# A two-block decoder on one core: expert gates made for 128 second keys at once, in groups of 4 tokens

## The reference, cut to what matters

```
choice:  128 triples (n1, n2, g) for each token: 8 heads x 16, g the softmax share
y[t]  =  sum over the triples of  g * gelu(h[t] . down[n1, n2]) * up[n1, n2]
x     =  x + y
```

## Time and profile before

| | us |
|---|---|
| median of three runs | 2606.18 (2598.7 to 2606.22) |
| the profiled execution | 2596.85 |
| its span | 2594.8 |
| PE busy | 2501.0 (96%) |
| DVE busy | 1346.8 (52%) |
| ACT busy | 418.4 (16%) |
| POOL busy | 237.9 (9%) |
| moved by DMA | 642.19 MB, mean 247 GB/s |

### The profile page before, as it was taken

How to read it: one execution, slowest core, us unless ns; L and a number is a source line. 1 busy time by engine, 2 the same in 40 slices (tenths; PEclk the granted TensorE clock), 3 DMA queues, 4 the chain that set the end, 5 groups by cost and what they waited for, 6 DMA issues and landing times.

```text
span 2594.8 us, 36855 instructions
## 1 busy us (share of the span) xinstructions
PE 2501.0 (96%) x15378; PEld 2095.0 (81%) x15378; DVE 1346.8 (52%) x2630; ACT 418.4 (16%) x1206; POOL 237.9 (9%) x256
## 2 busy tenths in 40 slices
PE   8999999999998899999999999889999999999998
PEld 7558999999988765699999999878666677776665
DVE  5825788888744385188888785434500010451001
ACT  2121121110110122122211011102100000430000
POOL 0000113222211000002311121100000000000000
PEclk9999999999999999999999999999999999889999
DMA  5314899999999522269999999983244342003443
GB/s 217 130 41 155 316 359 401 403 407 418 420 421 421 210 98 97 88 221 391 361 418 408 405 412 421 421 333 128 114 147 161 129 182 110 2 1 116 160 145 113
DMA packets 88103, 642.19 MB, mean 247 GB/s; under 512 B 11739, under 2 KB 14274, under 8 KB 15502
## 3 DMA queue, kind: packets, MB, share of 16 engines
q1 hardware_dynamic: 55596, 420.85, 41.9%
q0 software_dynamic: 31360, 218.33, 20.6%
q10 hardware_dynamic: 994, 0.82, 0.1%
HBM read 638.69 MB, written 1.06 MB: 247 GB/s over the span
## 4 chain that ended last, share of the span: by engine, by line
PE 63%; DMA 20%; DVE 11%; issue 4%; ACT 1%; DVEq 0%; SPq 0%; POOL 0%; POOLq 0%; PEldq 0%; ACTq 0%
DMA arena<-in_expert_rows,choice_by_pair 20%; PE bank L764 13%; PE bank L514 9%; PE bank L528 9%; PE bank L536 8%; PE bank L479 4%; DVE arena L1636 4%; PE bank L491 3%; PE bank L789 2%; PE bank L896 2%; DVE arena L1623 2%; PE bank L441 1%; DVE weight_ring L1741 1%; PE bank L945 1%; PE bank L445 1%
## 5 line engine op out<-in xcount | busy, mean ns | idle before, releaser
L789 PE MATMUL bank<-arena,weight_ring 128*128 128x152 f32 x4096 | 551.1, 294 | 24.4 <-DMA weight_ring<-in_experts 24.2
L789 PEld LDWEIGHTS bank<-arena,weight_ring 128*128 128x128 f32 x4096 | 532.9, 190 | 38.1 <-DMA weight_ring<-in_experts 34.5
L764 PE MATMUL bank<-hidden_T,weight_ring 128*128 128x152 f32 x4096 | 540.9, 293 | 9.3 <-ACT arena L1136 9.3
L764 PEld LDWEIGHTS bank<-hidden_T,weight_ring 128*128 128x128 f32 x4096 | 531.3, 190 | 11.8 <-issue 11.7
L1623 DVE CUSTOM_DVE_ANT_0 arena<-arena 128x1024 f32<-128x1024 f32 x208 | 254.4, 1223 | 237.3 <-DMA arena<-in_expert_rows,choice_by_pair 236.8
L1011 POOL DMA_INDIRECT arena<-in_expert_rows,choice_by_pair x208 | 211.1, 1015 | 849.9 <-DVE arena L1636 802.5
L1636 DVE SCALAR_TENSOR_TENSOR arena<-arena,pair_weights 128x1024 f32<-128x1024 f32 x202 | 258.8, 1281 | 0.2
L514 PE MATMUL bank<-hidden_T,weight_ring 128*128 128x256 f32 (+1 forms) x1088 | 240.5, 381 | 7.9 <-DVE hidden_T L1328 7.6
L528 PEld LDWEIGHTS bank<-hidden_T,weight_ring 128*128 128x128 f32 x1024 | 194.4, 190 | 55.0 <-issue 28.7
L1781 DVE TENSOR_TENSOR weight_ring<-weight_ring 128x256 f32<-128x256 f32 x64 | 27.2, 425 | 402.2 <-ACT weight_ring L1195 402.2
L514 PEld LDWEIGHTS bank<-hidden_T,weight_ring 128*128 128x128 f32 (+1 forms) x1088 | 201.5, 187 | 41.6 <-DVE hidden_T L1328 9.1
(11 more groups left out here) (328 smaller groups left out, 2046.6 us busy)
## 6 DMA issues: line engine op xcount, KB each, us to landing
weight_ring<-in_experts SPq DMA_DIRECT2D x256, 1024.0 KB, 9.8
weight_ring<-in_mlp SPq DMA_DIRECT2D x64, 1024.0 KB, 4.8
weight_ring<-in_dense_h SPq DMA_DIRECT2D x22, 2048.0 KB, 8.0
weight_ring<-in_dense_nsa SPq DMA_DIRECT2D x9, 2048.0 KB, 8.5
weight_ring<-in_dense_rg SPq DMA_DIRECT2D x7, 2048.0 KB, 7.7
arena<-in_expert_rows,choice_by_pair POOLq DMA_INDIRECT x208, 11.5
arena<-distance_bias_scratch SPq DMA_DIRECT2D x2, 768.0 KB, 6.3
residual<-in_x SPq DMA_DIRECT2D x1, 1024.0 KB, 5.4
```

What stands on the lines that cost most here:

```text
L764: last = mm(bank[s % 2][:, 0:DT_TOK], w[:, k * P:(k + 1) * P], HT[:, k, 0:DT_TOK], start=k == 0, stop=k == KD - 1)
L789: last = mm(bank[4 + k // 2][:, (k % 2) * DT_TOK:(k % 2 + 1) * DT_TOK], w[:, k * P:(k + 1) * P], HACT[:, s, :], start=s == 0 and k % 2 == ...
```

## The change

The gates of a token are made for all 128 second keys at once. A group is 4 tokens (GROUP), so there are 38 groups instead of 2 x 19, and each fills one PSUM bank (4 x 128) as before (8 x 64). All of them are placed between the rows of the first matrix: group n follows row CUT[n] = 67 + 31 n // 20 (67, 68, 70, 71, 73, ... 124). None is left in the second matrix.

- Rows up to CUT[n] already lie in HACT when the group's product is ready: DVE multiplies them as before (`keep`).
- Rows still to come are not there yet. ACT copies their gates out of PSUM into HACT, at the place where those rows will lie (`gates_ahead`). When such a row is computed, ACT puts the gelu of the tokens gated so far into a small buffer LATE and the others into HACT directly (two activations for one), and DVE multiplies LATE with the gates that lie in HACT (`late`, 60 rows a layer).
- The one-hots are two comparisons on DVE (4 x 128 each); the multiplication with the shares moves to ACT, one activation for each token (`weigh_onehots`, 152 a layer). They have three buffers instead of two.
- The rows of the first matrix use three PSUM banks instead of two, and PE waits for what ACT has kept three rows back; gate groups use five banks instead of three.
- Tiles in the first matrix: one in every second row from 64 on (LATE_TILES, 32), in place of 34 by TILES_AT.
- The late gathering moves from rows 64 and 76 to 48 and 72 and, on ACT, from tiles 80 and 89 to 70 and 84; the fold from after row 120 to after row 124.

```diff
@@ -46,20 +46,20 @@
 DT_TOK = 152
 GT0, GT1, GT2 = 192, 160, 152
 HALF = NKEYS // 2
-GROUPS = DT_TOK // 8
+GROUP = 4
+GROUPS = DT_TOK // GROUP
 TILES0, TILES1, TILES2 = 64, 32, 8
 TILES = TILES0 + TILES1 + TILES2
 GBUF = 4
-GATE_AT = tuple(1 + 3 * n for n in range(GROUPS))
-HIDDEN_GATE_AT = tuple(4 + 3 * n for n in range(GROUPS))
+CUT = tuple(HALF + 3 + 31 * n // 20 for n in range(GROUPS))
+LATE_TILES = range(HALF, NKEYS, 2)
 ROUTE_ORDER = (1, 0)
 EARLY_TILES = 6
 EARLY_PAIR_AT = tuple(38 + 3 * n for n in range(EARLY_TILES))
 EXP_AT = (25, 56)
 CHOICE_AT = 62
-TILES_AT = [2, 2, 1, 2, 2] * 4 + [2, 2, 1, 2, 2] * 4
-LATE_ROWS_AT = HALF
-LATE_ROWS_PAIR = 80
+LATE_ROWS_AT = 48
+LATE_ROWS_PAIR = 70
 PAIRS = NKEYS
...
@@ -82,6 +82,26 @@
 
 def buffer_of(layer, i):
     return (i + 2 * layer) % RING
+
+
+def gated_before(s):
+
+    return GROUP * sum(c < s for c in CUT)
+
+
+def parts(s):
+    g = gated_before(s)
+    return (g > 0) + (g < DT_TOK)
+
+
+def kept(s):
+
+    return 2 + sum(parts(i) for i in range(s + 1)) + sum(c < s - 1 for c in CUT)
+
+
+def put_by(s):
+
+    return kept(s) + (s - 1 in CUT)
 
 
 class Chain:
@@ -243,8 +263,9 @@
         nrow = at6(48 + D)
         scratch = ring[:, 2 * SLOT:3 * SLOT]
         IT = scratch[:, 0:3 * DT_TOK].rearrange("p (w t) -> p w t", t=DT_TOK)
-        OH1 = scratch[:, 576:576 + 2048].rearrange("p (s t n) -> p s t n", s=2, n=P)
-        OH2 = scratch[:, 2624:2624 + 1024].rearrange("p (s t n) -> p s t n", s=2, n=HALF)
+        OH1 = scratch[:, 456:1992].rearrange("p (s t n) -> p s t n", s=3, n=P)
+        OH2 = scratch[:, 1992:3528].rearrange("p (s t n) -> p s t n", s=3, n=P)
+        LATE = scratch[:, 3528:3984].rearrange("p (s t) -> p s t", s=3)
         act_g = scratch[:, 768:1280].rearrange("p (s n) -> p s n", n=T)
         act_c = scratch[:, 1280:2304].rearrange("p (s n) -> p s n", n=T)
         SST = stat[:, 0:24]
...
@@ -371,13 +392,13 @@
                     sp.dma_start(ring[:, r * 2048:(r + 1) * 2048], load(i)).then_inc(S[f"step_loaded{r}"], 16)
                     if i == PAIRS // 2 + 16:
 
-                        sp.wait_ge(S["hidden_kept"], NKEYS + 2)
+                        sp.wait_ge(S["hidden_kept"], kept(NKEYS - 1))
                         sp.wait_ge(S["gated"], GROUPS)
                         clear(front_names[:len(front_names) // 2])
                     if i == PAIRS // 2 + 20:
                         clear(front_names[len(front_names) // 2:])
 
-                sp.wait_ge(S["gated"], 2 * GROUPS)
+                sp.wait_ge(S["late_gated"], NKEYS - 1 - CUT[0])
                 for b in range(SLOTS):
                     if b:
                         sp.wait_ge(S["step_used"], PAIRS // 2 - 4 + 2 * b)
@@ -751,31 +772,26 @@
                 peer(l)
 
             def peer(l):
-                gate_bank = lambda n: bank[(2, 3, 4)[n % 3] if n < GROUPS else (2, 3, 0)[n % 3]]
-
                 def hidden(s):
 
                     i, r = s // 2, buffer_of(l, s // 2)
                     pe.wait_ge(S[f"step_loaded{r}"], 16 * (i // RING + 1))
 
-                    pe.wait_ge(S["hidden_kept"], s + 1)
+                    pe.wait_ge(S["hidden_kept"], kept(s - 3) if s >= 3 else 2)
                     w = ring[:, r * 2048 + (s % 2) * 1024:r * 2048 + (s % 2 + 1) * 1024]
                     for k in range(KD):
-                        last = mm(bank[s % 2][:, 0:DT_TOK], w[:, k * P:(k + 1) * P], HT[:, k, 0:DT_TOK],
+                        last = mm(bank[s % 3][:, 0:DT_TOK], w[:, k * P:(k + 1) * P], HT[:, k, 0:DT_TOK],
                                   start=k == 0, stop=k == KD - 1)
                     last.then_inc(S["hidden_ready"], 1)
 
                 def gates(n):
 
-                    pe.wait_ge(S["onehots_ready"], n + 1)
-                    if n >= 3:
-
-                        pe.wait_ge(S["gated"], n - 2)
-                    if n >= GROUPS:
-
-                        pe.wait_ge(S["hidden_kept"], NKEYS + 2)
-                    for j in range(8):
-                        last = mm(gate_bank(n)[:, j * HALF:(j + 1) * HALF], OH1[:, n % 2, j, :], OH2[:, n % 2, j, :],
+                    pe.wait_ge(S["onehots_ready"], GROUP * (n + 1))
+                    if n >= 5:
+
+                        pe.wait_ge(S["gated"], n - 4)
+                    for j in range(GROUP):
+                        last = mm(bank[3 + n % 5][:, j * P:(j + 1) * P], OH1[:, n % 3, j, :], OH2[:, n % 3, j, :],
                                   start=True, stop=True)
                     last.then_inc(S["gates_product"], 1)
 
@@ -796,38 +812,35 @@
                     hidden(s)
                 pe.wait_ge(S["choice_ready"], 6)
...
                 for s in range(CHOICE_AT, HALF):
                     hidden(s)
-                n = 0
                 for s in range(HALF, NKEYS):
                     hidden(s)
-                    if s - HALF in HIDDEN_GATE_AT:
-                        gates(n)
-                        n += 1
+                    for n in range(GROUPS):
+                        if CUT[n] == s:
+                            gates(n)
 
                 pe.wait_ge(S["gated"], GROUPS)
-                for s in range(HALF):
-                    back(s)
-                    if s in GATE_AT:
-                        gates(n)
-                        n += 1
-                pe.wait_ge(S["gated"], 2 * GROUPS)
-                for s in range(HALF, NKEYS):
+                pe.wait_ge(S["hidden_kept"], kept(CUT[-1] + 2))
+                for s in range(NKEYS):
+                    if s > CUT[0]:
+
+                        pe.wait_ge(S["late_gated"], s - CUT[0])
                     back(s)
                     if s == LATE_ROWS_AT:
                         for k in range(KD):
...
-                    if s == LATE_ROWS_AT + 12:
+                    if s == LATE_ROWS_AT + 24:
...
-                    if s == NKEYS - 8:
+                    if s == NKEYS - 4:
 
                         pe.wait_ge(S["pair_added"], TILES)
                         for q in range(2):
@@ -1132,8 +1145,29 @@
 
                 def hidden(s):
 
+                    g = gated_before(s)
                     act.wait_ge(S["hidden_ready"], s + 1)
-                    A(HACT[:, s, :], bank[s % 2][:, 0:DT_TOK], ACT.Gelu_apprx_tanh).then_inc(S["hidden_kept"], 1)
+                    if g:
+                        if s - 3 > CUT[0]:
+
+                            act.wait_ge(S["late_gated"], s - 3 - CUT[0])
+                        A(LATE[:, s % 3, 0:g], bank[s % 3][:, 0:g], ACT.Gelu_apprx_tanh).then_inc(S["hidden_kept"], 1)
+                    if g < DT_TOK:
+                        A(HACT[:, s, g:DT_TOK], bank[s % 3][:, g:DT_TOK], ACT.Gelu_apprx_tanh).then_inc(S["hidden_kept"], 1)
+
+                def gates_ahead(n):
+
+                    act.wait_ge(S["gated"], n + 1)
+                    A(HACT[:, CUT[n] + 1:NKEYS, GROUP * n:GROUP * (n + 1)],
+                      bank[3 + n % 5][:].rearrange("p (t n) -> p n t", t=GROUP)[:, CUT[n] + 1:NKEYS, :], ACT.Copy).then_inc(
+                          S["hidden_kept"], 1)
+
+                def weigh_onehots(n):
+
+                    act.wait_ge(S["onehots_equal"], 2 * (n + 1))
+                    for j in range(GROUP):
+                        A(OH2[:, n % 3, j, :], OH2[:, n % 3, j, :], ACT.Copy,
+                          scale=IT[:, 2, GROUP * n + j:GROUP * n + j + 1]).then_inc(S["onehots_ready"], 1)
 
                 def pair(j):
 
@@ -1155,27 +1189,30 @@
...
                 act.wait_ge(S["routing_done"], 1)
                 for s in range(HALF, NKEYS):
                     hidden(s)
-                    if s < HALF + 2:
+                    for n in range(GROUPS):
+                        if CUT[n] == s - 1:
+                            gates_ahead(n)
+                    if s < HALF + 3:
+                        weigh_onehots(s - HALF)
+                    for n in range(3, GROUPS):
+                        if CUT[n - 3] + 2 == s:
+                            weigh_onehots(n)
+                    if s < HALF + 2 or s - 2 in LATE_TILES:
                         pair(j)
                         j += 1
-                    for back in (2, 3):
-                        n = (s - HALF - back - HIDDEN_GATE_AT[0]) // 3
-                        if s - HALF - back in HIDDEN_GATE_AT and TILES_AT[n] >= 4 - back:
-                            pair(j)
-                            j += 1
                 while j < TILES:
                     if j == LATE_ROWS_PAIR:
 
...
-                    if j == LATE_ROWS_PAIR + 9:
+                    if j == LATE_ROWS_PAIR + 14:
 
                         act.wait_ge(S["pair_rows"], 9)
                         for q in range(2):
@@ -1729,38 +1766,47 @@
                 dve.wait_ge(S["choice_T"], 3)
                 dve.sem_inc(S["routing_done"], 1)
 
-                gate_bank = lambda n: bank[(2, 3, 4)[n % 3] if n < GROUPS else (2, 3, 0)[n % 3]]
-
                 def onehots(n):
 
-                    g, half = n % GROUPS, n // GROUPS
```

(48 more changed lines are left out.)

8 lines of the change are left out of this document (4 added, 4 removed).

## The result

The new kernel takes 2606.77 us (median of 11 runs, 2597.6 to 2610.69), the kernel before 2599.02 us in the same comparison (11 runs, 2594.86 to 2606.22). The ratio is 1.003, its 95% interval 1.0018 to 1.0043: 7.75 us slower, where 11 faster was forecast. The profiled execution took 2609.3 us, its span is 2607.5. One run of all that follow, of e7, took 2842.33 us at a granted clock of 0.839; the ratios leave it out, and e7's median without it is 2582.61.

A forecast was written before the change was run, and what follows sets the result against it. Transfers of the expert rows were taken as the bound. Layer 1 at -4.0 and layer 2 at -8.2 gave -12.2, of which -11 was taken: median 2606.18 becomes 2595 us, own range 2588 to 2601, overall 2576 to 2612.

The forecast's parts named there:

- What bounds the kernel: From row 64 of the first matrix on, transfers are the scarce thing, at 396 to 421 GB/s; PE isn't.
- PE's gates and the first matrix: Gate groups cost 0.89 us each, 33.9 a layer; the second matrix starts at 540.4 instead of 544.6.
- the stayed waits: Rival, chance 0.20: ACT still makes PE wait in the first matrix, +4.2 a layer, 2603 us, no change.
- a slow DVE: Rival, chance 0.14: DVE becomes the first matrix's bound, +10 us a layer, 2615 us.
- The rival of the old pace: Chance 0.16: second-matrix tiles keep their old pace of 4.83 us, 8.5 us a layer, 2578 us.
- The cost bound of ACT's one-hot: In the first matrix, weighting a one-hot on ACT costs between 0.295 and 0.394 us, 0.39 taken.
- The last dot: The last tile's dot, ending the second matrix's stream, comes at 851 (+2.2) in layer 1, 1722.2 (+0.1) in layer 2.
- the forecast's sum of -12.2: Both layers' changes added: -4.0 in layer 1 and -8.2 in layer 2, of which -11 was taken.
- the count by dots: Second matrix, layer 1: dot 42 at about 550, then 61 tiles at 4.97 us, so last dot at 853.
- the count by bytes: Second matrix, layer 1: 129.9 MB left at 421 GB/s take 308 us, so last dot at 848.
- Two tiles fewer ahead cost about 18, the rest gives 16 back: Layer 1's last dot: fewer early tiles and smaller share cost 18; DVE's bubble, earlier start and first-matrix gain return 16.
- The tail: Layer end: three rows instead of seven behind the fold, -8.35 a layer; layer 1 pays +2.2 for a slow-clock fold.

The follow-up runs named there:

- e7: New kernel with the next stage's block held until the last dot, late weights held behind tiles, 34 first-matrix tiles instead of 32: 2582.84 us, ratio 0.9949.
- e11: New kernel with 34 late tiles instead of 32 in the first matrix and nothing else changed: 2581.77 us, ratio 0.9935.
- e1: New kernel with the next stage's first block issued only when the last pair tile has been dotted: 2591.45 us, ratio 0.9983.
- e10: New kernel with the next stage's block held until the last dot, fold behind row 127 and 34 first-matrix tiles: 2565.32 us, ratio 0.9877.
- e3: New kernel with 304 dead matmuls a layer added on PE in the second matrix: 2582.05 us, ratio 0.9944.
- e12: e10 with 304 dead matmuls a layer added on PE in the second matrix's first 56 rows: 2578.62 us, ratio 0.9928.

## Why the prediction was wrong, step by step

- **What bounds the kernel: right in the second matrix, not in the first.** The expert rows' stream decides the end; PE's saving of 32 us a layer did not come out. But the forecast also called the transfers the scarce thing from 371.7 on, and e11 put two more tiles through the first matrix in the same time.
- **PE's gates and the first matrix: right.** 0.89 us a group, the second matrix 299.95 us behind the first hidden row; 540.4 less 238.1 in the profile before was 302.3. Neither ACT nor DVE held it up, so the rivals of the stayed waits and of a slow DVE fell. The rival of the old pace fell too: from dot 43 to dot 101 a step took 5.00 us on average, not 4.83. The cost bound of ACT's one-hot (0.394) measured 0.400.
- **The last dot: wrong, and this is the step that failed.** Forecast 851 and 1722.2 are 612.9 and 612.8 behind the first hidden row; 622.2 and 622.0 came, 9.3 and 9.2 late. That is nearly all of the distance between the forecast's sum of -12.2 and the +7.5 at "end"; the tail gives the last 1 us. In layer 1 the count by dots was good to its first term (dot 42 at 312.5, forecast 311.9) and its steps (4.97). What was missing: 4.2 us for the last two steps beside the next stage's block (6.78 + 7.34 - 9.94), 2.2 us of single long steps of 5.8 and 6.3, and 2 us given away by averaging with the count by bytes. In layer 2 the same terms are 3.9, 3.4 (with a dot 42 that came 1.6 late) and 2. The forecast saw the cause: it named the block that row 119 would release. It booked it as bytes (with two weight pairs 2.4 MB, so 0.3 for the block) and not as a rival on the queue while tiles were still to come.
- **The count by bytes: short by 5 MB.** It had 129.9 MB left for the second matrix up to the last dot. The windows below (the new kernel, then e1; GB/s last) give 322.25 x 419 = 135.0 MB and 314.4 x 417 = 131.1. Weights and tiles up to there are the same in both, so the block is the difference, 3.9 MB ahead of the last dot for the 0.3 booked. Weights are in the same case: PE's ran ahead, and PE was done with row 124 at 849.6, 14 us before the last dot. A sum of bytes tells the end only if it is known which bytes pass before the piece that is waited for.

```profile
541.56:863.81 322.25, 275.77 (x2022) 262.40 (x2020) 153.37 (x192) 33.95 (x133) 59.19 (x62) 0.98 1.01 419
...
541.10:855.50 314.40, 275.93 (x2022) 262.46 (x2020) 153.48 (x192) 33.95 (x133) 58.23 (x62) 0.99 1.00 417
```

- **"Two tiles fewer ahead cost about 18, the rest gives 16 back": a trade that did not have to be made.** e11 shows both tiles fit in the first matrix at no price (second matrix at 299.9, e10 301.0), and that with them the change would have been 17.8 us faster than before.
- **The tail: right.** Forecast -6.15 and -8.35, measured -5.7 and -7.8 from the last dot to the end. Three rows took 6.47; the clock was granted at 0.50, the 1.2 GHz level, from the fold's start to about 873.2 and at 1.00, the 2.4 GHz level, in its last microsecond and in the rows behind, as taken. PE's wait was 18 us for the 10 forecast, which follows from the last dot.

Windows of the new kernel, the fold and the rows behind it, which answer to the earlier trace rows (clock third from the right):

```profile
868.00:870.00 2.00, 2.00 (x4) 0.19 (x4) 0.00 (x0) 0.00 (x0) 0.00 (x0) 0.50 0.00 0
...
874.30:880.00 5.70, 5.70 (x46) 5.70 (x45) 0.00 (x0) 0.00 (x0) 0.00 (x0) 1.00 0.00 0
```

- **Not settled:** what makes the single long steps, one or two of over 5.8 us in most layers of the kernels here (in e1 none is over 5.73). Whether holding weights could help at another distance than 25 tiles was not tried.

## What to carry to other kernels

When two streams share full DMAs, count the pieces of the one that the end waits for, at its share, and ask what each engine that gets faster will put on the queue beside them. A prefetch for the next stage is harmless if its bytes come behind the last awaited transfer; in e11 it could be issued 12.6 us ahead of that. Work freed on an engine off the path buys nothing by itself: here it began to pay when the early tiles were kept (2582 us for 2607), and most when the block was held and the fold moved into the wait as well (2565). Before a trade is accepted, look whether its price has to be paid at all.

## What the hardware showed that was not expected

- The split of the DMAs between two queues follows the size of what each has: tile steps of 7.34 us beside 16 KB a partition and 4.98 beside 8 KB, of the same bytes in all.
- DMAs at a busy share of 1.00 can still take more: 402 GB/s in the new kernel, 413 in e11, in the same 164.7 us of the first matrix.
- A transfer issued at 837.2 behind queued weights began to slow the other queue only some 12 us later.
- Some 33 us of dead matmuls a layer made the kernel 25 us faster in one version (e3) and 13 us slower in another (e12).
- The kernel before alone spreads from 2583 to 2617 us over 30 runs, so its median of three was good to no more than about 7 us.
